# Scan units of a hybrid SSD / Hyena / mLSTM + MoE kernel: fixed PSUM banks and a new order, and five smaller moves (router tables, ring loads, a halved Square, outputs on two queues)

## The reference

```
u  = modulated_norm(x, norm1_w, shift, scale) @ w_in
yc, ssd_ctx, ml_ctx = token_mixers(uc, p, ssd_zero, ml_zero, not last)   # SSD | Hyena | mLSTM
yl, _, _            = token_mixers(ul, p, ssd_ctx, ml_ctx, True)
x  = x + gate * (y @ w_out)
x  = x + gate2 * hier_moe(modulated_norm(x, norm2_w, ...))   # 4 groups x 8 experts, top 1 then top 2
```

```
seg    = exp(where(causal, cum_l - cum_s, -inf))
scores = (C @ B.T) * seg                 # SSD; the mLSTM has Q @ K.T and log_w
y      = scores @ xdt + (C @ entering) * exp(cum)
state  = state * decay + chunk_state
```

## Time and profile before

| | |
|---|---|
| median of 3 runs | 1441.06 us (1438.72 to 1442.49) |
| the profiled execution, its time | 1442.18 us |
| its span, first to last instruction | 1440.3 us |
| mean granted TensorE clock | 0.902 |
| busy: PE / DVE / ACT / POOL | 84% / 44% / 21% / 9% |

### The profile page before, as it was taken

One profiled execution on the slowest core, in us unless ns is written; L12 is line 12 of the kernel. 1 busy time (PEld: TensorE's weight loads), 2 busy tenths in 40 slices (PEclk: granted clock), 3 DMA queues, 4 the chain that ended last, 5 costly groups with the idle time before them and its releaser, 6 DMA issues. The chain is left out here.

```text
span 1440.3 us, 19707 instructions
## 1 busy us (share of the span) xinstructions
PE 1207.3 (84%) x7632; PEld 791.0 (55%) x7632; DVE 636.9 (44%) x1257; ACT 296.7 (21%) x600; POOL 128.2 (9%) x144
## 2 busy tenths in 40 slices
PE   3899999989999849898977569999979489888982
PEld 1444547976678735554444356568758355444541
DVE  3524763116793452343322174853474534333333
ACT  2302012244334211131111132122622200000001
POOL 0000000000000012222221100000000112222210
PEclk8899999988799859999999869999979599999996
DMA  8743132226451448999999835341652667999992
GB/s 283 202 130 117 59 103 88 65 97 205 135 193 51 161 131 320 400 386 380 384 378 377 315 138 176 117 132 58 234 197 91 233 245 311 384 386 397 390 387 112
DMA packets 148149, 322.18 MB, mean 224 GB/s; under 512 B 28443, under 2 KB 111448, under 8 KB 123864
## 3 DMA queue, kind: packets, MB, share of 16 engines
q1 hardware_dynamic: 136664, 305.13, 58.6%
q0 software_dynamic: 11392, 15.77, 3.3%
HBM read 321.11 MB, written 21.23 MB: 238 GB/s over the span
## 5 line engine op out<-in xcount | busy, mean ns | idle before, releaser
L633 PE MATMUL bank<-hT,ring 128*128 128x512 f32 (+1 forms) x544 | 206.0, 537 | 1.5 <-issue 0.8
L633 PE MATMUL bank<-ring,qkT 128*64 128x256 f32 x976 | 151.5, 407 | 35.7 <-DMA ring<-in_moe_w_up 17.7
L633 PE MATMUL bank<-ring,hT 128*128 128x256 f32 (+1 forms) x928 | 179.1, 347 | 1.5 <-DVE ysum L1689 1.5
L633 PEld LDWEIGHTS bank<-ring,hT 128*128 128x128 f32 x928 | 153.8, 193 | 20.2 <-issue 2.3
L633 PEld LDWEIGHTS bank<-hT,ring 128*128 128x128 f32 x544 | 104.2, 193 | 97.9 <-issue 91.1
L1689 DVE TENSOR_TENSOR xbc<-xbc,bank 64x256 f32<-64x256 f32 x65 | 27.5, 423 | 278.1 <-ACT xbc L1329 244.4
L633 PEld LDWEIGHTS bank<-ring,qkT 128*64 128x64 f32 x976 | 94.9, 146 | 66.2 <-issue 23.4
L633 PE MATMUL bank<-hT,qkT 128*64 128x256 f32 x496 | 94.1, 417 | 11.5 <-DMA hT<-in_moe_w_up 6.3
L1329 ACT ACTIVATE xbc<-bank 64x256 f32<-64x256 f32 x65 | 24.6, 378 | 376.1 <-PE bank L633 340.4
L1261 POOL DMA_INDIRECT pair_rows<-hyT,zotok x65 | 60.0, 923 | 422.2 <-DVE xbc L1695 392.5
L633 PE MATMUL bank<-xtok,qkT 128*64 128x256 f32 x256 | 68.4, 428 | 13.9 <-DMA zotok<-in_moe_w_up 9.9
(11 more groups left out here) (325 smaller groups left out, 1683.6 us busy)
## 6 DMA issues: line engine op xcount, KB each, us to landing
ring<-in_w_mod SPq DMA_DIRECT2D x40, 1024.0 KB
ring<-in_moe_w_down SPq DMA_DIRECT2D x31, 1024.0 KB
ring<-in_moe_w_up SPq DMA_DIRECT2D x31, 1024.0 KB
ring<-in_moe_w_gate SPq DMA_DIRECT2D x30, 1024.0 KB
ring<-in_w_in SPq DMA_DIRECT2D x22, 1024.0 KB
hT<-in_moe_w_gate SPq DMA_DIRECT2D x16, 1024.0 KB
hT<-in_moe_w_up SPq DMA_DIRECT2D x15, 1024.0 KB
hT<-in_moe_w_down SPq DMA_DIRECT2D x15, 1024.0 KB
```

The source lines that it names most:

```text
L633: return nc.tensor.matmul(o, a, b, start=s, stop=e, **k)
```

## The change

What is new, in the words of the code:

1. `product` can be given a bank, and waits then for the reader of the last occupant of that bank. In the units the banks are fixed: `w` 0 and 1, `qkcb` 2 and 3, the third `w` 4 + u in units 0 and 1 and otherwise 0, and it is issued behind `qkcb`; `ys` and `st` 4, `carried` 5 and 6, `mn` 7, modulations 0 and 1, `mod_vector` 6. All other products still go round.
2. Layer 0: `weights_of(0)` stands ahead of `token_major("o", (3,))` on TensorE, and `segments(0)`, `segments(1)` ahead of `o_rows(3)` on ScalarE, which from then on is one unit further ahead. VectorE's `scores` and `combine` are split, and the loop is scores(u+1, 0), ssd_sums(u), scores(u+1, 1), carried_sums(u), prep(u+1), next_state(u), mod_columns, ml_sums(u). `ys` waits for the first half of the scores only, `mn` for the second.
3. In layer 0 only tile 0's norm stays in the units (end of units 4, 5, 6); tile 1's comes behind them. `mixed(0)` stands behind `outputs_of(7)`. In layer 1 the norm of tile 3, that stood before combine(7), stands behind ml_sums(7).
4. The Square of x after the output projection is done in two halves, so one operation of VectorE adds the two sums.
5. The router's pair table is a product of its own (47 columns), ahead of that of the weights; 4 of the operations on the one-hots stand earlier, and 2 of those on the table are gone.
6. SyncE issues 2 ring loads of layer 1, not 4, ahead of the reads of `pair_rows`.
7. The last two output DMAs are issued by ScalarE.

```diff
-        products = []
+        occupant, turn = {}, [0]
...
 
-                    for _ in range(SLOTS):
+                    for _ in range(2):
...
-                for row in range(ROWS):
+                for row in range(ROWS if t == 0 else ROWS // 2):
...
+            def product(name, bank=None):
+
+                if bank is None:
+                    bank = turn[0] % BANKS
+                    turn[0] += 1
+                old = occupant.get(bank)
+                if old:
                     pe.wait_ge(*due(("read", old)))
                     if old[0] == "down":
                         pe.wait_ge(*due(("read left", old)))
-                return banks[n % BANKS]
+                occupant[bank] = name
+                at[("bank", name)] = bank
+                return banks[bank]
...
+                    both = [product(("qkcb", l, u, j), 2 + j) for j in range(2)]
...
+                    segment_rows(2, 4 + u if u < 2 else 0)
...
-                        token_major("zo"[n // NT], (n % NT,))
+                            pe.wait_ge(*due(("split", l)))
+                            pe.wait_ge(*due(("silu qk", l, 2)))
+                            weights_of(0)
+                        token_major("zo"[n // NT], (n % NT,), 6 if n == 2 * NT - 1 else None)
...
-                        b = product(("ys", l, u))
-                        pe.wait_ge(*due(("scores", l, u)))
+                        b = product(("ys", l, u), 4)
+                        pe.wait_ge(*due(("scores", l, u, 0)))
...
-                            both = [product(("carried", l, u, j)) for j in range(2)]
+                            both = [product(("carried", l, u, j), 5 + j) for j in range(2)]
...
-                        b = product(("mn", l, u))
+                        b = product(("mn", l, u), 7)
+                        pe.wait_ge(*due(("scores", l, u, 1)))
...
-                        b = product(("st", l, u))
+                        b = product(("st", l, u), 4)
...
-                pe.wait_ge(*due(("split", l)))
-                pe.wait_ge(*due(("silu qk", l, 2)))
-                weights_of(0)
+                if l:
+                    pe.wait_ge(*due(("split", l)))
+                    pe.wait_ge(*due(("silu qk", l, 2)))
+                    weights_of(0)
                 for u in range(len(units)):
                     if u + 1 < len(units):
                         weights_of(u + 1)
+                    outputs_of(u)
                     if (l, u) == (0, 7):
                         mixed(0)
-                    outputs_of(u)
...
-                        modulation(*part)
+                            mod_vector(*vector, 6)
+                    for n, part in enumerate(mods_of_unit(l, u)):
+                        modulation(*part, n % 2)
...
-                b = product(("tables", l))
+                b = product(("pair table", l))
+                for y in range(2):
+                    pe.wait_ge(*due(("pair hot", l, y)))
+                    for t in range(t0, NT):
+                        last = mm(b[:, 0:ITEMS], slot_hot[:, y * NT + t, :], item_hot[:, y * NT + t, 1, :],
+                                  (y, t) == (0, t0), (y, t) == (1, NT - 1))
+                last.then_inc(pe_done, made(("pair table", l)))
+                b = product(("weight table", l))
+                pe.wait_ge(*due(("weight hot", l)))
                 combos = [y * NT + t for y in range(2) for t in range(t0, NT)]
                 for n in combos:
-                    pe.wait_ge(*due(("one-hot", l)))
-                    last = mm(b[:, 0:2 * ITEMS], slot_hot[:, n, :], item_hot[:, n, :, :], n == combos[0], n == combos[-1])
-                last.then_inc(pe_done, made(("tables", l)))
+                    last = mm(b[:, 0:ITEMS], slot_hot[:, n, :], item_hot[:, n, 0, :], n == combos[0], n == combos[-1])
+                last.then_inc(pe_done, made(("weight table", l)))
...
+                            decay_columns()
+                            segments(0)
+                            segments(1)
+                        (z_rows, o_rows)[n // NT](n % NT)
...
-                    act.wait_ge(*due(("x attended", l, t)))
-                    fn(xn_v[:, t, :], x_v[:, t, :], ACT.Square, ("ss", l, 2, t), accum_out=small[:, t:t + 1])
+                    for half in range(2):
+                        act.wait_ge(*due(("x half", l, t, half)))
+                        c_ = slice(512 * half, 512 * half + 512)
+                        fn(xn_v[:, t, c_], x_v[:, t, c_], ACT.Square, *([("ss", l, 2, t)] if half else []), scale=D ** -0.5,
+                           accum_out=small[:, 8 * half + t:8 * half + t + 1])
...
+            act.wait_ge(*due(("result", 1)))
+            for row in range(ROWS // 2, ROWS):
+                c0 = row * GRID_W + P // ROWS
+                act.dma_start(out[0, c0:c0 + P // ROWS, :], xn_v[row::ROWS, 1, :]).then_inc(out_written, 16)
...
 
-                scores(0)
+                scores(0, 0)
+                scores(0, 1)
                 prep(0)
                 last_unit = len(units) - 1
                 for u in range(len(units)):
                     if u < last_unit:
-                        scores(u + 1)
-                    if l == 0 and u == 5:
+                        scores(u + 1, 0)
+                    ssd_sums(u)
+                    if u < last_unit:
+                        scores(u + 1, 1)
+                    carried_sums(u)
+                    if u < last_unit:
+                        prep(u + 1)
+                    next_state(u)
+                    if u:
+                        for vector in vectors_after(mods_of_unit(l, u - 1)):
+                            mod_columns(*vector)
+                    ml_sums(u)
+                    if (l, u) == (0, 4):
                         gated(0)
                         head_squares(0)
-                    if l == 0 and u == 6:
+                    if (l, u) == (0, 5):
                         mix_inverse(0)
-                        gated(1)
+                    if (l, u) == (0, 6):
                         normed(0)
-                    if l == 0 and u == last_unit:
-                        head_squares(1)
-                        mix_inverse(1)
                     if l and u == last_unit:
                         gated(3)
                         head_squares(3)
                         mix_inverse(3)
                         normed(3)
-                    if u < last_unit:
-                        prep(u + 1)
-                    combine(u)
-                    if u:
-                        for vector in vectors_after(mods_of_unit(l, u - 1)):
-                            mod_columns(*vector)
                 for vector in vectors_after(mods_of_unit(l, u)):
                     mod_columns(*vector)
                 if l == 0:
+                    gated(1)
+                    head_squares(1)
+                    mix_inverse(1)
...
-                        tt(x_v[:, t, cs_], x_v[:, t, cs_], attended, ADD, *([("x attended", l, t)] if half else []))
+                        tt(x_v[:, t, cs_], x_v[:, t, cs_], attended, ADD, ("x half", l, t, half),
+                           *([("x attended", l, t)] if half else []))
                     if n:
                         logits(order[n - 1])
                     dve.wait_ge(*due(("ss", l, 2, t)))
-                    ts(small[:, 4 + t:5 + t], small[:, t:t + 1], 1.0 / D, EPS, MUL, ADD)
+                    stt(small[:, 4 + t:5 + t], small[:, t:t + 1], EPS, small[:, 8 + t:9 + t], ADD, ADD)
...
                        ALU.is_equal)
+                    tt(item_hot[:, hot(y), 1, :], item_hot[:, hot(y), 0, :], wide(pair_no, hot(y), ITEMS), MUL, ("pair hot", l, y))
                 dve.wait_ge(*due(("r4", l)))
                 step(V.tensor_reduce(gsum[:, t0:], ge_v[:, t0:], AX.X, ADD))
                 stt(den[:, t0:], e2[:, t0:], 1.0, gsum[:, t0:], ADD, MUL)
                 step(V.reciprocal(den[:, t0:], den[:, t0:]))
                 tt(m2[:, t0:], den[:, t0:], e2[:, t0:], MUL)
                 for y, share in enumerate((den, m2)):
-                    tt(item_hot[:, hot(y), 0, :], item_hot[:, hot(y), 1, :], wide(share, slice(t0, NT), ITEMS), MUL)
-                    tt(item_hot[:, hot(y), 1, :], item_hot[:, hot(y), 1, :], wide(pair_no, hot(y), ITEMS), MUL, ("one-hot", l))
-
-                dve.wait_ge(*due(("made", ("tables", l))))
-                b = bank(("tables", l))
-                nowhere, later = room(ITEMS), room(ITEMS)
-                pairs = b[:, ITEMS:2 * ITEMS]
-                ts(nowhere, pairs, 0.5, NOWHERE, ALU.is_lt, MUL)
-                stt(nowhere, pairs, -1.0, nowhere, ADD, ADD)
-                ts(later, pairs, NT * P + 0.5, -1.0 * NT * P, ALU.is_gt, MUL)
-                tt(later, later, nowhere, ADD)
-                copy(token_of[:, 0:ITEMS], later, ("item tables", l))
-                copy(pair_of[:, 0:ITEMS], nowhere, ("pair table", l))
```

(11 more changed lines are left out.)

155 lines of the change are left out of this document (77 added, 78 removed).

## The result

The changed kernel takes 1424.61 us (1421.34 to 1429.08), before it is 1441.06: ratio 0.990, 95% interval 0.9871 to 0.9929, so 14 us faster by the ratio (the two medians lie 16.5 us apart). The forecast was 1428.5 with a range of 1417 to 1440.5. The profiled execution was the slowest of the five runs, 1429.08 us; it has a span of 1427.2 us against 1440.3.

A forecast was written before the change was run, and what follows sets the result against it. TensorE and VectorE, neither full, wait for each other in a ring in the units, with the clock falling behind waits. Terms -9 + 4 - 2.7 - 0.5 - 3.3 - 1.2 = -12.7 gave 1428.5 us, range 1417 to 1440.5.

The forecast's parts named there:

- Layer 0's units: Decay product to first output product in layer 0: -15 at full clock, plus 6 for half clock, so -9 us.
- The price of half clock: In layer 0's units each us at half clock costs 0.43 us, taken between 0.38 and 0.48.
- the last rival: Slower by fixed banks: TensorE's waits for bank readers within units hold the clock down; 1449.5 us at 63 us half clock, chance 0.10.
- The 3.40 us ahead of tile 3's transposes: TensorE's idle time behind layer 0's units, taken as not saved and set against output products starting at half clock.
- Layer 1's units: Same order but little room: first output product 1.2 us later, plus 2.8 for more half clock, +4 us.
- Router and Square: Router's more table 1.3 us earlier in layer 0, 1.4 in layer 1, -2.7; Square in halves -0.5 us.
- The sign that I gave for it: Router: more table would start 1.3 us earlier after the table product's start.
- Ring loads: Layer 0's last scatter to its read-back: two ring loads fewer ahead of it, -3.3 us.
- Outputs: End of the kernel: two fewer output DMA issues on SyncE's path, -1.2 us.
- the read-back: Layer 0: last scatter to read-back would be near 3 us, where it was 6.2.
- the six issues: End of the kernel: six output issues behind the last result, where there were eight.
- half-clock time: Layer 0's units: about 14 us at half clock, where before they were 41.

The follow-up runs named there:

- turns: Changed kernel with no fixed banks, all products in turn over the 8 banks, order kept; 1418.05 us, ratio 0.9843 to the old kernel.
- mixed_banks: Changed kernel with only the two products of tile 0's transposes moved from banks 7 and 0 to 2 and 3; ratio 0.9874 to the old kernel.
- no_tab: Changed kernel with the router's tables as in the old kernel, one product of 94 columns; ratio 0.9925 to the old kernel.
- units_only: Changed kernel with ring loads, outputs, router tables and Square undone, leaving fixed banks, new order and norms; ratio 0.9967 to the old kernel.
- small_only: Old kernel with only the small edits: router tables, halved Square, ring loads, two outputs on ScalarE's queue; ratio 0.9961 to the old kernel.
- again: Changed kernel without any edit, measured a second time on another occasion; 1424.63 us, ratio 0.9894 to the old kernel.

## Why the prediction came out right

Term by term, in the first trace (span -13.1; ahead of the units the kernel was already 1.8 earlier, by nothing that the change touches):

- **Layer 0's units**, put at -9: -8.9 by the table, -10.3 to the first `ring,hT` product, the event that the prediction names. The number is right, its two parts are not, and that they cancelled is luck. I laid out -15 at full clock and took 14 us at half clock, to come to -9. The trace has 29 us at half clock, so the bare schedule was better than I had laid out: turns, with 0.05 x 2 x 95.6 = 10 us at half clock, gained 16.5. The -10.3 are 4.3 by the earlier start (decay product to unit 0's `ys`, 15.5 before and 11.2 after), 12.5 in the seven cycles from there to unit 7's `ys` (91.3 and 78.8), and 6.6 lost behind it (3.97 and 10.57).
- **The price of half clock**, put at 0.43 us for each us: it is less firm than the prediction has it. Its 0.48 rests on a bare cycle of 10.8 us, where the text elsewhere has 10.3 and 10.4, and its 0.38 on units 4 to 6, which ran in part at half clock themselves. Turns against the changed kernel gives (103.2 - 95.6) over 19 us, 0.4. Traces with the same program up to unit 7 give 2.8 us for 6.9 (mixed_banks, 0.41) and 3.5 for 13.7 (no_tab, 0.25).
- **The cause of the 29 us** was sought in the last rival, waits within the units for the readers of fixed banks. That fixed banks go with them is shown: 7.7 us here, and not the 24 that would have turned the sign. That waits are the way is not: they add up to the same (9.3 and 9.0 us). The largest half-clock stretch ahead of unit 7, from 323 on, is in five of seven traces of this program, missing in mixed_banks and no_tab, and in none of the four with layer 0 in turn; without it the seven cycles take 75.3 and 76.0 us, against 74.4 to 75.0 in turn. The rule of the Trainium skill on cycling PSUM banks ("TensorE: Matmul & The Clock Gate", "A second HAM failure mode: psum-queue depth-cycling") agrees as far as small waits between groups stand ahead of the falls at 323 (1.49 us) and 391 (1.36); it doesn't tell the two allocations apart.
- **The 3.40 us ahead of tile 3's transposes** I set against other losses. It was saved: units_only, with no router edit, has 107.8 from the first output product to more table, 3.7 less than before, and in the changed kernel tile 3's transposes, at 421.20, wait for nothing. This is the term that I left out.
- **Layer 1's units**, put at +4: +1.9 with the input stage. The steps were right (late start by waits for ScalarE, 1.92 for the `o` rows; tile 3's norm late), but my layout had not seen that the products still in turn meet the fixed banks. With the counter elsewhere it is +5.1 to +6.8.
- **Router and Square**, put at -2.7 and -0.5: -0.9 in layer 0 and -2.4 in layer 1 by small_only, -3.3 in all. The tables alone are -1.2 and -1.1 in every trace, near the -1.3 and -1.4 of the sum. In layer 0 the 32 narrower matmuls take 7.03 us, 0.22 each, and the 16 wider ones before took 3.70, 0.23 each, both at a clock of 0.50: a product of half the columns costs nearly as much, as I had taken it. The sign that I gave for it was wrong: more table comes 1.9 us later after the table product's start (7.6 us, before 5.6), but that start is 3.1 us earlier.
- **Ring loads**, put at -3.3: -2.8 (6.2 to 3.4).
- **Outputs**, put at -1.2: -1.3, in every run that has the edit. Here the Trainium skill ("DMA: Bandwidth & Descriptors", "Issuing engines are not separate DMA queues") agrees: what went is two issues, and no more.
- **MoE**, not in the sum: +6.0 and +1.1. In one trace it ate nearly half of the gain ahead of it; by the run again and the 14 traces side by side it is the spread of the weight stream from run to run, not an answer to the change.

The errors went both ways: -3.7 and -2 that I had not counted, +7 of MoE and the 1.8 at the start that are chance. That the time is 4 us under the forecast is as near as these allow, and in part luck. Of the signs, the first output product (400.15, said about 402), unit 0's `ys` (4.3 us earlier after the decay product, said 5), the read-back (3.4) and the six issues came; half-clock time was twice what was said, and one wait of VectorE for its preparation is left (2.32 us at 327.66, unit 2).

What stays open is which wait, if any, sets off which fall of the clock: mixed_banks and no_tab have the same program as the changed kernel up to unit 7 and other half-clock stretches, with units 0 at 97.2 and 100.9. Nor was the new order taken apart: no run has the earlier start, the split scores and the moved norms one by one.

## What to carry to other kernels

Before banks are fixed for one loop, look at who reads each of them last, and at every product outside the loop that still takes its bank in turn: one product more or less elsewhere moved these onto other banks and was worth 3 to 5 us in layer 1's traces, more than most edits. Try a new order without fixed banks first: in layer 0's units this one gained 16 us in turn and 9 with fixed banks. Cut the trace into stages at fixed events and compare those, and take no event that the change itself makes wait. Then compare the places of the half-clock stretches ahead of the edit: where they differ with the same program, the stage differs by them too, here by up to 3.5 us.

## What the runs showed of the hardware

- The clock of TensorE fell in the same program at other places from run to run, and such a stretch moves a stage by some us: up to unit 7's `ys` 17.1, 10.2 and 3.4 us at half clock and 89.9, 87.1 and 86.5 us in all (changed, mixed_banks, no_tab). Layer 0's router ran its table matmuls wholly at 0.50, here after 6.59 us of idle time.
- At that clock fp32 matmuls with 128x128 weights took 0.22 us each with 47 columns and 0.23 with 94: their number counted, not their columns. TensorE was loading weights for nearly all of it: 6.88 us for the 32, 3.46 for the 16.
- With two ring loads issued ahead of it, the read-back of the last scatter's rows was issued 3.0 to 3.4 us after the scatter's start, with four 5.6 to 6.2, with none (layer 1) 2.5.
- The stage from the first rows copy to the last scatter of layer 0, in which the DMA engines were 95% busy (before) and 93% (changed), varied by 6 us over 14 traces.
